# A hybrid diffusion step with mixture of experts: features tile by tile, weights laid out by ring slot, zero matmuls and squares by group at the stage edges

## What is computed

```python
def layer(x, cond, l, p, ctx):
    mod = jnp.einsum('...d,de->...e', jax.nn.silu(cond), p['w_ada'][l]) + p['b_ada'][l]
    sh1, sc1, g1, sh2, sc2, g2 = jnp.split(mod.reshape(-1, 1, 6 * D_MODEL), 6, axis=-1)
    hn = rmsnorm(x, p['norm_mix'][l]) * (1.0 + sc1) + sh1
    mix, ctx_tensors = token_mixers(hn, l, p, ctx)
    x = x + g1 * mix
    hn = rmsnorm(x, p['norm_ffn'][l]) * (1.0 + sc2) + sh2
    x = x + g2 * moe(hn, l, p)
```

## Time and profile before

| | |
|---|---|
| median of 3 runs | 1043.91 us (1043.82 to 1045.93) |
| the profiled execution | 1044.16 us |
| its span in the trace | 1042.3 us |
| TensorE busy | 962.6 us (92%) |
| VectorE, ScalarE, GpSimd busy | 427.8, 171.9, 58.8 us |
| mean granted TensorE clock | 0.965 |
| bytes moved | 303.65 MB, mean 291 GB/s |

### The profile page before, as it was taken

How to read it: one execution, slowest core, us unless ns; L and a number is a source line. 1 busy time by engine, 2 the same in 40 slices (tenths; PEclk the granted TensorE clock), 3 DMA queues, 4 the chain that set the end, 5 groups by cost and what they waited for, 6 DMA issues and landing times.

```text
span 1042.3 us, 13821 instructions
## 1 busy us (share of the span) xinstructions
PE 962.6 (92%) x5404; PEld 531.1 (51%) x5404; DVE 427.8 (41%) x771; ACT 171.9 (16%) x436; POOL 58.8 (6%) x92
## 2 busy tenths in 40 slices
PE   5999998999789999999979999889997999999996
PEld 2755564558644444443447456545784444434442
DVE  1385875442422221222237689554224222222222
ACT  1212033320201010100020201532031101000100
POOL 1112220010000000000000223000000000000000
PEclk9899998999789999999989999989898999999999
DMA  9977564558259999999963765523452999999993
GB/s 372 363 280 286 205 242 162 207 165 302 81 218 421 421 421 421 421 421 421 417 248 123 269 224 200 197 87 102 155 212 92 423 422 421 421 422 420 421 421 126
DMA packets 68015, 303.65 MB, mean 291 GB/s; under 512 B 7808, under 2 KB 18064, under 8 KB 39152
## 3 DMA queue, kind: packets, MB, share of 16 engines
q1 hardware_dynamic: 61952, 291.52, 70.7%
q0 software_dynamic: 2960, 8.63, 2.3%
q10 hardware_dynamic: 3040, 2.62, 0.8%
HBM read 300.10 MB, written 2.65 MB: 290 GB/s over the span
## 4 chain that ended last, share of the span: by engine, by line
PE 82%; DVE 10%; ACT 3%; issue 2%; DMA 1%; SPq 0%; DVEq 0%; ACTq 0%
PE ps L407 80%; PE ps L440 2%; ACT eP L1475 2%; DMA ring<-in_w_ada 1%; DVE A L1156 1%; DVE sq L1123 1%; DVE rt L975 1%; DVE stat L975 1%; DVE xy L1150 1%; DVE t L1455 1%; DVE x L1458 1%; DVE t L1195 0%; DVE proj L1183 0%; DVE proj L1125 0%; DVE proj L1196 0%
## 5 line engine op out<-in xcount | busy, mean ns | idle before, releaser
L407 PE MATMUL ps<-ring,proj 128*64 128x512 f32 x1536 | 339.4, 595 | 8.8 <-issue 6.8
L407 PEld LDWEIGHTS ps<-ring,proj 128*64 128x64 f32 x1536 | 109.8, 137 | 214.9 <-issue 212.9
L407 PE MATMUL ps<-ring,hnT 128*128 128x512 f32 (+1 forms) x576 | 210.7, 520 | 7.4 <-ACT kd L1487 5.4
L407 PEld LDWEIGHTS ps<-ring,hnT 128*128 128x128 f32 x576 | 110.6, 197 | 88.4 <-issue 73.1
L407 PE MATMUL ps<-hnT,ring 128*64 128x256 f32 (+2 forms) x768 | 87.8, 353 | 1.8 <-DVE hnT L1039 1.8
L407 PEld LDWEIGHTS ps<-hnT,ring 128*64 128x64 f32 (+1 forms) x768 | 67.6, 151 | 19.7 <-issue 3.5
L407 PEld LDWEIGHTS ps<-proj,xs 128*128 128x128 f32 x512 | 62.5, 203 | 16.3 <-issue 16.3
L407 PE MATMUL ps<-proj,xs 128*128 128x128 f32 x512 | 65.5, 290 | 4.2 <-issue 4.2
L407 PE MATMUL ps<-ring,silT 128*32 128x512 f32 x384 | 51.6, 659 | 11.3 <-DVE silT L990 7.4
L407 PE MATMUL ps<-proj 128*128 128x512 f32 x128 | 61.5, 606 | 0.0
L1445 DVE COPY proj<-ps 128x512 f32<-128x512 f32 x16 | 11.1, 691 | 108.9 <-PE ps L407 108.9
(11 more groups left out here) (221 smaller groups left out, 767.0 us busy)
## 6 DMA issues: line engine op xcount, KB each, us to landing
ring<-in_w_gate SPq DMA_DIRECT2D x64, 1024.0 KB, 13.6
ring<-in_w_up SPq DMA_DIRECT2D x64, 1024.0 KB, 12.2
ring<-in_w_down SPq DMA_DIRECT2D x64, 1024.0 KB, 11.4
ring<-in_w_ada SPq DMA_DIRECT2D x48, 1024.0 KB, 9.2
ring<-in_w_in SPq DMA_DIRECT2D x28, 1024.0 KB, 7.2
ring<-in_w_out SPq DMA_DIRECT2D x16, 512.0 KB, 3.6
ring<-in_w_in SPq DMA_DIRECT2D x4, 512.0 KB, 14.8
xy<-gates POOLq DMA_DIRECT2D x4, 512.0 KB, 5.3
```

Of the source, the lines that this page charges most:

```text
L407: ins = nc.tensor.matmul(*a, **k)
```

## The change

Features are split as (k p): tile k is the contiguous block of features 128k to 128k+127, in x, xs, modX, act, in the small parameters and in the weights. The host lays out w_in, w_out, w_gate, w_up and w_down so that each ring load is one contiguous block, with one run per partition. w_ada keeps its layout. modulation_by_feature uses eight matmuls of 128 stationary columns instead of sixteen of 64. For layer 1 it moves from ahead of layer 0's normalized("hn2") to the wait for the picks, in bank 1, with VectorE's part behind line 1391. stream_zeros(b, n) issues n bfloat16 matmuls of zeros of 512 columns into bank b at the edges; zero is also cleared by VectorE at the start. The last squares of group 0 in layer 1 wait for its own rows of x only. VectorE takes three of the four banks in shifted, ScalarE the last.

The loads on SyncE:

```diff
-                        load(lambda s: ring[:, s:s + 1, :, 0:n], w_in[:, one(l), KH * r:KH * (r + 1), col:col + n])
+                        size = P * KH * n
+                        at = D * IN_AT[name] + r * size
+                        load(lambda s: flat_slot(s)[:, 0:KH * n], ap["w_in"][l, at:at + size].rearrange("(p m) -> p m", p=P))
...
-                        load(lambda s: ring[:, s:s + 1, :, 0:256], w_out[:, one(l), KH * r:KH * (r + 1), i * 256:(i + 1) * 256])
+                        load(lambda s: flat_slot(s)[:, 0:KH * 256], ap["w_out"][l, i, r])
...
-                                    load(lambda s: ring[:, s:s + 1], w[:, one(l * NE + t * 2 + e), KH * half:KH * (half + 1)])
+                                    load(flat_slot, half_experts[w][:, 2 * (l * NE + t * 2 + e) + half])
```

On TensorE, zeros and normalization:

```diff
+            def stream_zeros(b, n):
+                for _ in range(n):
+                    mm(ps[:, b, :], zeros[:, 0:P], zeros[:, 0:BLK], start=True, stop=True, skip_group_check=True)
+            def claim_for_norm():
+                b = (0, 3)[n_tr[0] % 2]
+                n_tr[0] += 1
+                pe.wait_ge(S(f"bank{b}_free"), c.claim(b))
+                return b
-            def normalized(stage, factors):
+            def normalized(stage, factors, ahead=(0, 0), first=None):
                 for g in range(NG):
-                    pe.wait_ge(c.of(factors, g), c.at(factors, g))
-                    xv = x[:, g].rearrange("p (q k) -> p k q", k=KC)
+                    xv = x[:, g].rearrange("p (k q) -> p k q", k=KC)
                     for h in range(2):
-                        b = (0, 3)[n_tr[0] % 2]
-                        n_tr[0] += 1
-                        pe.wait_ge(S(f"bank{b}_free"), c.claim(b))
+                        b = claim_for_norm() if first is None else first
+                        first = None
+                        if not h:
+                            stream_zeros(b, ahead[g])
+                            pe.wait_ge(c.of(factors, g), c.at(factors, g))
```

modulation_by_feature, and the calls of normalized for the two layers' first stage:

```diff
-                    mv = modX[:].rearrange("p (q k) -> p k q", k=KC)
                     for k in range(KC):
-                        for h in range(2):
-                            last = mm(ps[64 * h:64 * h + 64, b, 4 * k:4 * k + 4], mv[:, k, :], C["pickm"][:, 4 * h:4 * h + 4], start=True, stop=True)
+                        at, h = P * (k % KH), k // KH
+                        last = mm(ps[:, b, 4 * k:4 * k + 4], modX[:, at:at + P], C["pickm"][:, 4 * h:4 * h + 4], start=True, stop=True)
...
                 if l == 0:
+                    b = claim_for_norm()
                     for step in EARLY[0:5]:
                         ada_step(*step)
+                        stream_zeros(b, 3)
                     pe.wait_ge(c.of("begin_dma"), c.at("begin_dma"))
-                    normalized("hn1", "xn1")
+                    normalized("hn1", "xn1", first=b)
...
-                    normalized("hn1", "xn1")
+                    normalized("hn1", "xn1", (14, 0))
```

In by_head_and_group, ahead of normalized("hn2"), in the loop over the router's groups, and ahead of the picks:

```diff
+                    if not l:
+                        stream_zeros(b, 5)
...
-                if l + 1 < L:
-                    modulation_by_feature(l + 1, 0, 2)
-                normalized("hn2", "xn2")
+                normalized("hn2", "xn2", (0, 3))
...
+                    stream_zeros(b, 3 * g)
...
+                if l + 1 < L:
+                    modulation_by_feature(l + 1, 0, 1)
+                pe.wait_ge(S("bank2_free"), c.claim(2))
+                stream_zeros(2, 8 if l + 1 < L else 18)
                 pe.wait_ge(c.of("picks", 0), c.at("picks", 0))
-                pe.wait_ge(S("bank2_free"), c.claim(2))
```

shifted on VectorE; squares and shifted on ScalarE:

```diff
-                    for h in range(2):
+                    for g, h in ((0, 0), (0, 1), (1, 0)):
...
-                            acte.wait_ge(S("x2"), c.before("x2"))
+                            acte.wait_ge(S("x2"), c.before("x2") - (NG - 1 - g if l else 0))
...
-                    for h in range(2):
+                    for h in (1,):
```

More of the change, by code:

```diff
@@ L292, in build, with flat_slot, by_k @@
         zeros = zero.bitcast(mybir.dt.bfloat16)
+        def flat_slot(s):
+            return ring[:, s].rearrange("p k n -> p (k n)")
+        def by_k(s, n):
+            return flat_slot(s)[:, 0:KH * n].rearrange("p (k n) -> p k n", n=n)
         def tok(g):
@@ L383, in _ @@
                         led.turn = t
-                        for w in (w_gate, w_up):
+                        for w in ("w_gate", "w_up"):
                             for half in range(2):
                                 for e in range(2):
-                                    load(lambda s: ring[:, s:s + 1], w[:, one(l * NE + t * 2 + e), KH * half:KH * (half + 1)])
+                                    load(flat_slot, half_experts[w][:, 2 * (l * NE + t * 2 + e) + half])
                         for half in range(2):
                             for e in range(2):
-                                load(lambda s: ring[:, s:s + 1].rearrange("p o k n -> p o (k n)").rearrange("p o (k n) -> p o k n", k=KE // 2),
-                                     w_down[:, one(l * NE + t * 2 + e), KE // 2 * half:KE // 2 * (half + 1), :])
+                                load(flat_slot, half_experts["w_down"][:, 2 * (l * NE + t * 2 + e) + half])
                     led.where = "rounds"
@@ L548, in by_head @@
                                 col = 64 * h + (256 * d if name == "f" else 0)
-                                last = mm(ps[64 * d:64 * d + 64, b, 256 * hl:256 * (hl + 1)], ring[:, ss[k // KH], k % KH, col:col + 64], hnT[:, k, :], start=(k == 0), stop=(k == KC - 1), skip_group_check=True)
+                                last = mm(ps[64 * d:64 * d + 64, b, 256 * hl:256 * (hl + 1)], by_k(ss[k // KH], 512 if name == "f" else 256)[:, k % KH, col:col + 64], hnT[:, k, :], start=(k == 0), stop=(k == KC - 1), skip_group_check=True)
                                 if not (hl and k == KC - 1 and d):
@@ L924, in _ @@
                         pe.wait_ge(c.of("act"), c.at("act"))
-                        bank_of_transposes(("actT",), [act.rearrange("p (q k) -> p k q", k=KE)[:, k, :] for k in range(KE)], 0)
+                        bank_of_transposes(("actT",), [act[:, k * P:(k + 1) * P] for k in range(KE)], 0)
                         if t:
@@ L983, in _ @@
             st(v.memset(silT[:].rearrange("p k n -> p (k n)"), 0.0))
+            st(v.memset(zero, 0.0))
             st(v.memset(s0r[:].rearrange("p r h e -> p (r h e)"), 0.0), "s0r_zero")
@@ L1819, in packed, with laid_out @@
     return {n: np.ascontiguousarray(a, dtype=np.float32) for n, a in out.items()}, packs
+def laid_out(inputs):
+    halves = lambda a, k: a.reshape(*a.shape[:-2], 2, k, P, a.shape[-1]).swapaxes(-3, -2)
+    w_in = np.asarray(inputs["w_in"])
+    out = {"w_in": np.concatenate([halves(w_in[:, :, col:col + n], KH).reshape(L, -1) for _, col, n in IN_BLOCKS], 1)}
+    w_out = np.asarray(inputs["w_out"]).reshape(L, D, 4, 256).transpose(0, 2, 1, 3)
+    out["w_out"] = halves(w_out, KH).reshape(L, 4, 2, P, KH * 256)
+    for n in ("w_gate", "w_up"):
+        out[n] = halves(np.asarray(inputs[n]), KH).reshape(L, NE, 2, P, KH * DE)
+    out["w_down"] = halves(np.asarray(inputs["w_down"]), KE // 2).reshape(L, NE, 2, P, KE // 2 * D)
+    return {n: np.ascontiguousarray(a, dtype=np.float32) for n, a in out.items()}
 _OUTS = [("o_yp", (1, P, D)), ("o_ys", (1, P, D)), ("o_k", (1, L, P, NH, 2, DQ)), ("o_v", (1, L, P, NH, DV)),
```

40 lines of the change are left out of this document (19 added, 21 removed).

## The result

| | before | changed |
|---|---|---|
| median of 5 runs | 1043.91 us (1043.35 to 1045.93) | 1039.05 us (1033.60 to 1039.30) |
| the profiled execution | 1044.16 us | 1033.60 us |
| its span | 1042.3 us | 1031.8 us |
| mean granted TensorE clock in it | 0.965 | 0.972 |

The ratio is 0.9933, with a 95% interval of 0.9915 to 0.9951: faster by 0.7%, 4.9 us of the forecast 20, and outside the range of 1017 to 1034. In the table, the brackets hold the lowest and the highest run. The profiled execution was the fastest of the five, by luck of the clock, as the first experiment shows. The other four took 1038.66 us at a mean clock of 0.969 and 1039.05, 1039.24 and 1039.30 at 0.965.

The account below looks back on a forecast made before the run. TensorE was taken to bind, with the expert loops at the transfers' pace, so only gains ahead of turn 0 count. Terms 6.1+5.8+4.1+3.6+0.4 = 20.0 us off 1044.16 gave 1024.2, stated as 1024.0 us, range 1017 to 1034.

Parts of the forecast that it names:

- Contiguous loads: Normalizing products on x: 32 take 3.84 us instead of 7.92 once weight loads read contiguous features.
- the boundary: Between layers 0 and 1: group 0's squares no longer wait for group 1, products start earlier; 4.1 us gained.
- The term 2.8 for layer 0: Layer 0, normalization to router's end: earlier start, pace set by PSUM banks; 272.4 instead of 275.2, 2.8 us gained.
- layer 1's stretch: Layer 1, normalization to router's end: start unchanged, router done at 778.0 instead of 779.1; 1.2 us gained.
- The start: Kernel start to f's end: earlier modulation steps 3.6 us, modX 0.2, f at full clock 2.3; 6.1 us gained.
- The gathers: First gather of each layer at full clock, 3.84 us: 2.5 us gained in layer 0, 1.6 in layer 1.
- The products with the picks: Ahead of each gather, at half clock before: 0.9 us gained in layer 0, 0.85 in layer 1.
- the clock is not held: Rival, chance 0.19: zeros fail at f, gathers, picks and boundary; 12.7 us lost, time 1037, or 1030 if half.
- the moved copy: Layer 0's normalization: the third bank copy, moved to VectorE, is hidden behind other work, costing nothing.
- the rest within the mixers: Half-wide modulation and stepped transposes inside the mixers: 0 to 2 us gained, taken as 0.4.
- Slower: Rival, chance 0.05: expert loads dislike their new places; at 400 GB/s a turn is 31.4 us, time 1049.
- better: Rival, chance 0.03: the expert load rate rises, turns go down to 29.36 us; 4.8 us less, 1019.

Follow-up runs that it names:

- the first experiment: The changed kernel run again as it is, six runs: median 1037.28 us (1031.79 to 1039.82), ratio 0.9923 to the kernel before.
- stepped_x: The changed kernel, but its first normalization of each layer reads x with the old step of eight floats: 1037.31 us, one run.
- no_zeros: The changed kernel with all 72 streams of zeros left out: median 1035.19 us, ratio 0.9905 to the kernel before.
- params_late: The changed kernel without the five zeros ahead of f, GpSimd's parameter loads held until f's first bank is full: 1030.59 us, ratio 0.9875 to the kernel before.
- zeros_first: The changed kernel with layer 0's five f zeros ahead of the wait for f's ring slots: 1031.55 us, ratio 0.9885 to the kernel before.
- gather_zeros: The changed kernel without the five zeros ahead of f, with eight zeros between pick products and gather: 1030.45 us, ratio 0.9864 to the kernel before.
- the longer execution: The profiled run when the changed kernel was timed again unchanged: 1039.77 us, against 1033.60 us for the changed kernel's earlier profiled run.
- weights_as_given: The changed kernel, but w_in, w_out and expert weights read from where they stand in the inputs, in shorter runs: 1067.12 us, one run.
- together: params_late plus gather_zeros, without zeros in the normalization stretches and the router: 1028.76 us, ratio 0.9844 to the kernel before.

## Why the prediction was wrong

**Direction and bound: right.** TensorE's chain with the expert loops at the transfers' pace held: turns of layer 0 start at 355.98, 385.96 and 415.80 us, 29.98 and then 29.84 apart, and everything gained ahead of turn 0 was passed on whole.

**Contiguous loads: right.** 3.84 was forecast for 32 products and 3.96 came, and stepped_x shows the step to be the cause. The Trainium skill (TensorE: Matmul & The Clock Gate, LDWEIGHTS (loading the stationary operand)) has the load's time from its columns alone. This case's loads of 128 float32 columns took 335 ns with the step and 191 without, so here the measurement decides against that rule.

**Stretches paced by banks, and the boundary: right.** The term 2.8 for layer 0 came as 2.8. It came as two halves: the products follow the start of the last add by 0.89 us instead of 2.32 (the modulation moved away, 1.4), and the stretch to the router's end shrank from 12.38 to 11.04 (1.3). Its three zeros in each group cost 0.9 of what could be had, as no_zeros shows; I had counted them in. The boundary came to 4.0 of 4.1, layer 1's stretch to 1.15 of 1.2.

**The start: the step that failed most, 6.1 forecast and 1.1 had.** Three links of it broke. First, "its weights (2 MB more, at 26.6 + 5) are there when it starts at 32": they landed at 33.6, since I divided only the bytes that are waited for by the full rate. The trace before held the answer: there the eighth modulation load landed at 26.5, and the second load of f, issued at 15.7, 17.6 us later, at 33.3, two loads in 6.8 us and not 5. It went unseen since f's input, at 35.8, came later still.

```profile
L354 SPq DMA_DIRECT2D ring<-in_w_in x1: 373/373/373, 15.7 to 15.7; - x1
...
DMA to landing us min/median/max: 17.6/17.6/17.6
```

params_late puts some 0.7 of the two missing us on GpSimd's parameters; 0.58 MB of the ring's own other loads fits the rest. Second, the five zeros "run while its input is made": they stand behind the wait for the ring slots in program order, so they began only when the weights were there, and added some 2.2 us. I read the place of stream_zeros within by_head_and_group and not that of open_block ahead of it. Third, "finds the clock up": at 31 it was at half, and the zeros, at half clock themselves, did not bring it back before f, which took 15.2 us and not 14.1. zeros_first, which mends the second alone, gives back 2.2 of these.

**The gathers: the term that fell second.** "The gather gains 2.5 if the 8 zeros keep the clock" and 1.6 in layer 1: measured 0.5 and a loss of 1.05 (5.45 to 6.50 us). The zeros stand ahead of the picks, and between them and the gather lie a wait of 0.8 to 1.3 us, 1.6 us of small products and a wait of 1.9 to 2.4 us in which the rounds are read. Dense zeros up to the wait for the picks did not hold the clock past that second wait (it fell at 280.5 and 778.8 us), and gather_zeros, with zeros in it, got 3.90 and 3.83. The products with the picks came out better than forecast; they run at full clock, and from them to the gather 1.1 and 1.3 us gained for the 0.9 and 0.85 forecast.

**The rival "the clock is not held": half true, and too narrow.** It had the places f, gathers, picks and boundary, and 1037 us for the case that all are lost. Held were the boundary (in the longer execution but for 0.2 us) and the picks; lost were f and the gathers. My argument against it, the clock at 1.00 through the pause of 278.0 to 282.7, stopped the reading a tenth of a us too early, for the same trace has it at half from 282.8, straight behind that pause:

```profile
282.70:287.77 5.07, 2.77 (x12) 2.38 (x13) 2.57 (x14) 0.59 (x1) 0.00 (x0) 0.51 0.00 0
```

What took the longer executions to 1039 was in none of its places: 5.5 of their 6.1 us (by the longer trace) lie between f and the normalization in the two layers. The change does not touch the waits there, and the executions lose these us or keep them. I argued from one profile before, at 0.965, as if its clock were the kernel's; the range left no room for that.

**Costed at nothing, rightly:** the moved copy in layer 0 and the expert turns. The loads of w_in and w_out were costed at nothing too, which no run tested by itself; in weights_as_given f's last load landed at 34.3 us instead of 33.6. **Costed at 0.4 and not seen:** the rest within the mixers, where the profiled execution took 0.2 and 0.4 us more than the one before. **Slower and better** fell: the rate stayed at 421 GB/s with the pieces back to back.

Left open: why the clock falls in the mixers in some executions and not in others, whether it does so more often in the changed kernel, and how the ring's loads share their queue at the start. Zeros within the mixers' waits were not tried.

## What to carry to other kernels

Place filler matmuls by program order: behind no wait that the next real block has too, and in the very last wait ahead of the work that should run fast; fillers ahead of a short block do not carry the clock over the pause behind it, and in a stretch that another engine or the transfers pace they only cost. Price an arrival by all bytes that the queues have under way, not by those waited for, and look up when the same load landed in the trace before, also where something later hid it. Before judging a change of a few us on a kernel with gaps, look at the mean clock of several executions of each side: here runs of one kernel spread over 8 us with the clock, more than the 4.9 us of the change.

## What the runs showed of the hardware

- The time of one and the same kernel on one core goes with its mean granted clock: eleven runs of the changed kernel from 1031.79 us at 0.976 to 1039.82 at 0.965.
- bfloat16 matmuls of zeros count as work for the clock. With three behind each of the first five modulation steps, the steps went at full clock from the third on (1.06 or 1.07 us, nine traces); without, they stayed at 1.94 up to the fourth (three traces). The gather of layer 1 straight behind eight at full clock took 3.83 us in both traces that have them, without them 6.2 to 6.7 in eight traces of the changed kernel and its variants and 3.83 in one. Behind eight that ran at half clock nearly from their start the gather of layer 0 took 3.90 and, in together, 4.23. Five begun at half clock (2.29 us) did not bring the clock back for f.
- A stationary operand read with a step of eight floats costs the load 335 ns instead of 191; 32 products on it take 7.67 us instead of 3.96 (stepped_x).
- Reading the experts' weights in 2 KB and 4 KB runs, from where they stand in the inputs, gave 391 to 394 GB/s against 421 with 8 KB runs, in the expert loop, where the ring's queue alone moved data (0.1 MB of others in 300 to 520 us).
